# The order of a decoder layer's first splits, some of them on GpSimd, and its last output unit in two halves of 256 columns

## What is computed

```python
h = rmsnorm(x, norm_pre_g)                      # (512, 1024)
u = h @ w_in                                    # (512, 4096): dq, dk, dv, dg, mq, mk, mv, mg, 512 columns each
a = subln(diff_attention(dq, dk, dv)) * silu(dg)   # 4 heads, two softmax maps each, relative bias
b = moba_attention(mq, mk, mv) * silu(mg)          # 8 heads, two blocks of 256, relative bias
y = concat(a, b) @ w_out                        # (512, 1024)
out = x + rmsnorm(y, norm_post_g)
```

## Time and profile before

| | |
|---|---|
| Median of 3 runs | 281.91 us (280.83 to 282.24) |
| Profiled execution, first to last instruction (span) | 280.6 us |
| TensorE busy | 269.3 us, 96% |
| DVE, ScalarE, GpSimd busy | 174.4, 142.8, 29.3 us |
| Granted TensorE clock, mean | 0.994 |

### The profile page before, as it was taken

One profiled execution on the slowest core, in us unless ns is written; L12 is line 12 of the kernel. 1 busy time (PEld: TensorE's weight loads), 2 busy tenths in 40 slices (PEclk: granted clock), 3 DMA queues, 4 the chain that ended last, 5 costly groups with the idle time before them and its releaser, 6 DMA issues.

```text
span 280.6 us, 4661 instructions
## 1 busy us (share of the span) xinstructions
PE 269.3 (96%) x1669; PEld 140.0 (50%) x1669; DVE 174.4 (62%) x383; ACT 142.8 (51%) x335; POOL 29.3 (10%) x76
## 2 busy tenths in 40 slices
PE   6699999999999999999999999999999999999991
PEld 6455444444435555555545445555555565564440
DVE  2685734356777767776876686654687675654423
ACT  2975433266445665557456646574545536442200
POOL 2165000000000000050050130050000000001101
PEclk9999999999999999999999999999999999999997
DMA  7992994258754332204306535224001340101003
GB/s 220 386 317 82 357 386 159 82 139 304 225 188 120 97 99 60 77 7 151 111 2 199 138 112 149 77 78 112 1 2 37 119 183 2 75 2 71 5 25 124
DMA packets 26410, 35.65 MB, mean 127 GB/s; under 512 B 10496, under 2 KB 12808, under 8 KB 26388
## 3 DMA queue, kind: packets, MB, share of 16 engines
q1 hardware_dynamic: 26388, 35.37, 39.0%
HBM read 29.04 MB, written 2.13 MB: 111 GB/s over the span
## 4 chain that ended last, share of the span: by engine, by line
PE 67%; DVE 16%; ACT 9%; issue 4%; DMA 2%; POOL 1%; SPq 0%; DVEq 0%; POOLq 0%; ACTq 0%
PE unit_ps L529 55%; ACT arena L704 4%; PE pt_ps L565 4%; DVE w_lo L785 3%; PE o_ps L583 3%; DVE w_lo L783 2%; DVE pt_lo L880 2%; DMA stage<-in_w_in_dram 2%; PE score_ps L546 2%; DVE arena L854 2%; ACT pt_hi L714 2%; DVE arena L873 2%; PE score_ps L550 2%; PE o_ps L596 1%; ACT junk L643 1%
## 5 line engine op out<-in xcount | busy, mean ns | idle before, releaser
L529 PE MATMUL unit_ps<-w_hi,area 128*128 128x512 f16 x256 | 81.4, 380 | 2.4 <-DVE area L843 1.7
L529 PE MATMUL unit_ps<-area,w_hi 128*128 128x512 f16 x256 | 76.2, 380 | 0.1
L704 ACT ACTIVATE arena<-arena,negmax 128x512 f32<-128x512 f32 (+3 forms) x64 | 35.4, 553 | 61.0 <-DVE negmax L854 61.0
L529 PE MATMUL unit_ps<-area,w_lo 128*128 128x512 f16 x128 | 48.5, 379 | 0.0
L529 PE MATMUL unit_ps<-w_lo,area 128*128 128x512 f16 x128 | 48.5, 379 | 0.0
L880 DVE TENSOR_TENSOR pt_lo<-pt_ps,pt_hi 128x512 f16<-128x512 f32 (+5 forms) x32 | 21.0, 657 | 43.5 <-ACT pt_hi L714 43.5
L529 PEld LDWEIGHTS unit_ps<-w_hi,area 128*128 128x128 f16 x256 | 25.0, 98 | 33.1 <-issue 3.4
L529 PEld LDWEIGHTS unit_ps<-area,w_hi 128*128 128x128 f16 x256 | 24.1, 98 | 26.9 <-issue 0.3
L783 DVE SCALAR_TENSOR_TENSOR w_lo<-stage,g_cols,w_hi 128x512 f16<-128x512 f32 x32 | 25.0, 781 | 7.2 <-ACT w_hi L657 7.1
L854 DVE CUSTOM_DVE_ANT_0 arena<-score_ps,strips 128x512 f32<-128x512 f32 (+3 forms) x64 | 28.5, 482 | 0.0
L529 PE MATMUL unit_ps<-w_hi,q_hi 128*128 128x512 f16 x64 | 24.3, 380 | 0.0
(11 more groups left out here) (84 smaller groups left out, 350.3 us busy)
## 6 DMA issues: line engine op xcount, KB each, us to landing
stage<-in_w_in_dram SPq DMA_DIRECT2D x32, 512.0 KB, 4.5
stage<-in_w_out_dram SPq DMA_DIRECT2D x8, 512.0 KB, 4.3
strips<-bias_rows SPq DMA_DIRECT2D x1, 3072.0 KB, 12.4
arena<-in_x_dram SPq DMA_DIRECT2D x4, 512.0 KB, 8.8
q_twice<-q_hi SPq DMA_DIRECT2D x32, 64.0 KB, 2.7
k_pair<-gates SPq DMA_DIRECT2D x32, 64.0 KB, 2.7
stage<-in_x_dram SPq DMA_DIRECT2D x1, 2048.0 KB, 7.8
out_dram<-area SPq DMA_DIRECT2D x3, 512.0 KB, 2.6
```

Source lines behind the costliest of these rows:

```text
L529: last = nc.tensor.matmul(bank, a, b, start=(k == 0 and n == 0), stop=(k == KT - 1 and n == 2))
L704: nc.scalar.activation(probs[:, i % 2, m, 0:n], neglog[:, i % 2, m, 0:n], ACT.Exp, bias=negmax[:, i, m:m + 1], scale=-1.0, accum_out=sums[ ...
```

## The change

Four things, each within the diff below.

1. ScalarE and DVE do tile 0's `x_hi` and `x_lo` ahead of `split(0)`.
2. GpSimd writes the upper halves of quarters 1 and 3 (`split_hi_part`: two tensor_scalar of 128x512 each), behind its `x_rstd` of tile 0 and tile 1; ScalarE no longer does.
3. ScalarE's `x_hi(1)` moves ahead of `x_square(2)`, and DVE's `x_lo(1)` ahead of `split(3)`.
4. Unit 39 is done as two halves of 256 columns, each 24 matmuls into a bank of `score_ps`, with a square and a weighting for each, and one more small add on GpSimd.

```diff
+    HALF_COLS = WIDTH // 2
+    POOL_SPLITS = [1, 3]
...
+            def split_hi_part(n):
+                g, k = n // 4, 2 * (n % 4)
+                pool.wait_ge(g_scaled, 1)
+                pool.wait_ge(w_loaded[n % 4], 16 * (n // 4 + 1))
+                src = stage[:, n % 4, :].rearrange("p (k n) -> p k n", k=2)
+                for half in range(2):
+                    last = nc.gpsimd.tensor_scalar(w_hi[:, g % 3, k + half, :], src[:, half, :],
+                                                   g_cols[:, k + half:k + half + 1], 1.0, ALU.mult, ALU.mult)
+                last.then_inc(pool_split_hi, 1)
...
                 nc.gpsimd.tensor_tensor(x_rstd[:, t:t + 1], x_ms[:, t:t + 1], minus_half[:, 0:1],
                                         ALU.pow).then_inc(x_rstd_ready, 1)
+                if t < len(POOL_SPLITS):
+                    split_hi_part(POOL_SPLITS[t])
...
+                if t == 0:
+                    pool.wait_ge(y_squared, 2 * TILES + 1)
+                    nc.gpsimd.tensor_tensor(y_last_ms[:, :], y_last_sq[:, :], y_ms[:, 0:1],
+                                            ALU.add).then_inc(y_mean, 1)
+                    pool.wait_ge(y_mean, TILES + 1)
+                    nc.gpsimd.tensor_tensor(y_rstd[:, 0:1], y_last_ms[:, :], minus_half[:, 0:1],
+                                            ALU.pow).then_inc(y_rstd_ready, 1)
+                    break
...
+            def last_unit():
+                _, _, i, g = unit_of(UNITS - 1)
+                pe.wait_ge(logits_ready, 2 * NSTEP)
+                pe.wait_ge(at_ready, 2 * TILES)
+                pe.wait_ge(split_lo, 4 * (g + 1))
+                for half in range(2):
+                    cols = slice(half * HALF_COLS, (half + 1) * HALF_COLS)
+                    for k in range(KT):
+                        wh, wl = w_hi[:, g % 3, k, cols], w_lo[:, g % 3, k, cols]
+                        ah, al = at_hi[:, i % 2, k, :], at_lo[:, i % 2, k, :]
+                        for n, (a, b) in enumerate(((ah, wh), (ah, wl), (al, wh))):
+                            last = nc.tensor.matmul(score_ps[:, half, 0:HALF_COLS], a, b,
+                                                    start=(k == 0 and n == 0), stop=(k == KT - 1 and n == 2))
+                    last.then_inc(last_half_done, 1)
...
             for u, q in FILL_LAST:
-                unit_quarter(u, q)
+                if u < UNITS - 1:
+                    unit_quarter(u, q)
+            last_unit()
...
+                if u == UNITS - 1:
+                    for half, dst in enumerate((y_sq[:, i, r:r + 1], y_last_sq[:, :])):
+                        act.wait_ge(last_half_done, half + 1)
+                        square(dst, score_ps[:, half, 0:HALF_COLS], y_squared, u - IN_UNITS + 1 + half)
+                    return
...
             x_square(0)
-            split(0)
             x_hi(0, 0)
             x_hi(0, 1)
-            split(1)
+            split(0)
             x_square(1)
             split(2)
-            split(3)
+            x_hi(1)
             x_square(2)
-            x_hi(1)
             x_square(3)
...
-                dve.wait_ge(split_hi, n + 1)
+                if n in POOL_SPLITS:
+                    dve.wait_ge(pool_split_hi, POOL_SPLITS.index(n) + 1)
+                else:
+                    dve.wait_ge(split_hi, n + 1 - sum(m < n for m in POOL_SPLITS))
...
+                if u == UNITS - 1:
+                    for half in range(2):
+                        dve.wait_ge(y_squared, u - IN_UNITS + 1 + half)
+                        ycols = slice(r * WIDTH + half * HALF_COLS, r * WIDTH + (half + 1) * HALF_COLS)
+                        nc.vector.tensor_tensor(y_sb[:, i % 2, ycols], score_ps[:, half, 0:HALF_COLS], g_row[:, ycols], ALU.mult)\
+                            .then_inc(y_weighted, 1)
+                    return
...
-            split(0)
             x_lo(0, 0)
             x_lo(0, 1)
+            split(0)
             split(1)
             x_norm(1)
             split(2)
+            x_lo(1)
             split(3)
             x_norm(2)
-            x_lo(1)
             x_norm(3)
```

More of the change, by code:

```diff
@@ L229, in bass_hymba_diff_moba_layer @@
         y_ms = sb("y_ms", [P, TILES])
+        y_last_sq = sb("y_last_sq", [P, 1])
+        y_last_ms = sb("y_last_ms", [P, 1])
         y_rstd = sb("y_rstd", [P, TILES])
@@ L265, in bass_hymba_diff_moba_layer @@
         split_lo = sem("split_lo")
+        pool_split_hi = sem("pool_split_hi")
         consts_ready = sem("consts_ready")
@@ L277, in bass_hymba_diff_moba_layer @@
         unit_done = sem("unit_done")
+        last_half_done = sem("last_half_done")
         unit_read = sem("unit_read")
@@ L916, in finish_rows @@
                 parts = 1 if t else 2
-                dve.wait_ge(y_weighted, 2 * (i + 1))
+                dve.wait_ge(y_weighted, 2 * (i + 1) + (t == 0))
                 dve.wait_ge(y_rstd_ready, i + 1)
```

## The result

The changed kernel took 284.87 us (median of 4 executions, 283.58 to 287.61) against 281.77 before (median of 4): a ratio of 1.0127, 95% interval 1.0094 to 1.0161. The ratio is that of the means (285.23 and 281.65); the medians alone give 1.0110. It is slower, as forecast, but by nearly twice the size: +3.1 us between the medians, where +1.75 was forecast, and by the ratio twice the forecast 283.7 / 281.91 = 1.0063. The median is inside the whole forecast range (281.4 to 285.0), and above the 283.2 to 284.5 of the forecast's own case (A). The four executions come in two kinds, and their mean granted clocks tell which: 283.58 and 284.07 at 0.996 and 0.997, 285.67 and 287.61 at 0.990 and 0.986. The profiled execution is the 285.67 one; its span is 283.9.

A forecast was written before the change was run, and what follows sets the result against it. TensorE sets the time in the long middle, leaving only start and tail open. +2.0 at the start - 0.22 at the tail gave about +1.75 on the 280.6 span, 282.4, plus 1.3 to the median: 283.7 us, range 281.4 to 285.0.

The forecast's parts named there:

- (A): The prediction's own case for the whole kernel: slower, 283.2 to 284.5 us; chance 0.50.
- chain in front of q3: At the start, T1, x_hi(1), x_lo(1) and split(3) run one behind the other: 4.7 us from T1 to q3.
- q3: Last of the four quarters of unit 0 on TensorE; forecast to start at 19.15 and take 1.3 us.
- T1: Transposes of x's tile 1 on TensorE, between unit 0's second and third quarters; forecast at 14.4, as before.
- (D): Rival: the clock falls in the new gap ahead of q3 at the start; 285.0 us or so, chance 0.08.
- q0: First of the four quarters of unit 0 on TensorE; forecast to start at 11.4 with GpSimd and DVE contending.
- collisions: At the start, GpSimd's split_hi_part and DVE's w_lo or x_norm wait for each other, taking back the 0.8 us at T1.
- head start: At the start, without contention, T1 would come at 13.6, 0.8 us earlier than before.
- The tail: Behind the last matmul, ScalarE squares 256 columns instead of 512: gain 0.22 us, between 0 and 0.3.
- (B): Rival: GpSimd and DVE don't meet at the start; +1.1 - 0.22, 282.8 us, chance 0.17.
- (C): Rival: T1 comes at 13.6 and q3 isn't late; -0.8 - 0.22, 280.8 us, chance 0.10.
- (E): Rival: the start's delay is absorbed, leaving only the tail's gain and noise; 281.7 us, chance 0.15.

The follow-up runs named there:

- both stands filled: Changed kernel with 16 warm-up matmuls instead of 8 and split(3) ahead of x_lo(1) on DVE: 283.07 us against 282.42 before, ratio 1.0035.
- the one ahead of q0 filled alone: Changed kernel with 16 warm-up matmuls instead of 8 behind tile 0's transposes: 283.98 us against 282.18 before, ratio 1.0087.
- the one ahead of q3 shortened alone: Changed kernel with split(3) ahead of x_lo(1) on DVE: 282.79 us against 282.18 before, ratio 1.0039.
- GpSimd's halves alone: Kernel before with only the upper halves of quarters 1 and 3 moved from ScalarE to GpSimd: 282.69 us against 282.42, ratio 1.0020.
- x first alone: Kernel before with only tile 0's x_hi and x_lo ahead of split(0) on ScalarE and DVE: 282.03 us against 282.42, ratio 0.9993.

## Why the prediction was right in its mechanism and short in its size

**The chain in front of q3: right, and it is the whole constant loss.** T1 to q3 was 4.73 for 4.7, T1 to unit 1 6.91 for 6.95. The moves of `x_hi(1)` and `x_lo(1)` alone give 6.97, and 284.03 against 282.34. Swapping the one pair on DVE back in the changed kernel takes 1.2 us off.

**The step that failed: T1 at 14.4 "as before", at a full clock.** The prediction took the clock to be at 1.00 until the tail. Its rival (D) saw a fall only in the gap between q2 and q3, with a chance of 0.08, and it didn't price the other stand, the one ahead of q0. Its own walk put q0 at 11.4, some 2 us behind the last warm-up, and it said nothing of that; the kernel before had stood 1.7 us there at a full clock. In the profiled execution the stand became 2.08, the clock was 0.50 from 12.0 to 15.3, and T1 came at 15.86, 1.4 us late. At most 0.8 of that is the clock (T1's input was ready at 15.08); the other 0.6 is `x_norm(1)`, held up by x_rstd and by GpSimd's half in an execution whose loads landed 0.6 to 0.7 us later than before. So two of the signs named were missed, T1 between 13.6 and 14.9 and unit 1 between 20.5 and 21.9 (22.77); the gap ahead of q3, 2.16, was in its range. Four of ten executions show a lower mean clock and lie 1.0 to 3.6 us above the median of the other six; the medians' difference of 3.1 us, where 1.75 was forecast, is this and the scatter of four executions.

**What is shown of the clock, and what isn't.** That a longer stand ahead of q0 makes a lower mean oftener is shown in the kernel before (7 of 12 executions without the warm-ups, 4 of 90 with them). In the changed kernel it is 4 of 10, and 0 of 12 with both stands filled; with the one ahead of q0 filled alone it is 1 of 6, with the one ahead of q3 shortened alone 2 of 12 (one of them at 0.993). The long stand ahead of q3 in the old kernel gives 1 of 16 (both runs of that pair). That points to the stand ahead of q0, but it doesn't separate the two in the changed kernel. Where the stand ahead of q0 is 1.71 in the profile, with x first and no halves on GpSimd, it is 0 of 30 (three runs). One run doesn't fit: GpSimd's halves alone, with the old order up to q0, gave 3 of 12. Only one execution with a fall in the start was profiled, and it also had later landings, and those can delay T1 by themselves (at a full clock, with the changed order up to T1, it is at 13.64 where tile 1 landed 6.7 us behind its issue, and at 14.11 and 14.25 where that took 7.4; here it took 8.3). No run holds the landings fixed, so how much of the 1.0 to 3.6 us is the clock stays open. An estimate for the slowest execution: 0.986 against the 0.997 of the others over 285.8 us is 3.1 us of full-speed time, so even there the clock need not be all of the 3.6.

**GpSimd against DVE: the rule right, its weight too large.** 0.69 for 0.75 each, turns taken as forecast, `x_norm(1)` held up as forecast. But the prediction gave the collisions 0.9 of its 2.0 us, and taking GpSimd out of the changed kernel won 0.2. The walk through the queues used one execution's landings; in another the first pair ran before DVE wanted the port. The prediction also said that ScalarE's relief "buys little", and it is worth about what the collisions cost.

**The constant part: right in size, in part by luck.** It is +1.8 for +1.75, and the chain gives 1.93 us by itself (6.91 against 4.98). At T1 the prediction set a head start of 0.8 against collisions that ate it. The head start is there at the landings that it went by (13.72 for 14.43, without GpSimd), but it turns into a loss at earlier ones, and x first alone is 0.9993 of the time of before; the collisions net of ScalarE's relief are 0.2. The two errors go against each other. Two sums of the prediction are slightly off and change nothing: the floor for T1 adds up to 12.94, not 12.98, and the gap ahead of q3 by its own walk is 19.15 - 16.2 - 1.3 = 1.65, not 1.8.

**The tail: right.** Forecast -0.22, in the profile 0.18 less 0.08. Too small for the time to show.

**The rivals.** (B), no collision, would be 282.8, and isn't it: at a full clock without GpSimd the time was 283.8. (C), the head start wins, is out, as T1 to unit 1 never fell below 6.9 with `x_lo(1)` in front. (E), absorbed, is out by the same runs. (D) had a fall of the clock, but in the gap ahead of q3; in the one fall profiled it came behind q0's stand, and the clock was 1.00 from 16.98 to 20.59.

## What to carry to other kernels

When a wait is moved forward in an in-order queue, count what stands behind it: `x_lo(1)` was ready to be made earlier and wasn't needed before unit 1, but in front of `split(3)` it made q3 wait for a transpose, a copy and a subtraction of another tile. A change that makes a stand of TensorE a few tenths longer should be priced with the lower clock behind it as well as without (one stand of 2.08 us had it, one of 2.93 didn't), and the mean granted clock of each execution read beside its time, since the median can hide two kinds. And a walk through the queues worked out from one execution's landings holds for that execution; the distance between two steps of one queue, T1 to unit 1, held: 4.98 or 4.97 in all five undisturbed profiles with the old order behind T1 and no halves on GpSimd, 6.91 or 6.97 in all five with the new one.

## What the runs showed of the hardware

A tensor_scalar of 128x512, float32 to float16, takes GpSimd 0.69 us alone, a little less than DVE's `w_lo` of the same size. Side by side the two engines took turns by the instruction, each instruction that waited at 1.1 to 1.2 us. And the clock at the start isn't the same in every execution: in the repeated run of the changed kernel the transposes of tile 0 took 1.97 us and the warm-ups behind them 2.75, instead of 1.09 and 1.95. The clock record of that execution begins 10.3 us into the span, and that of the kernel before at 4.4, so the rise to the full clock came later there; the windows before the record's start read 1.00, and the mean of 0.995 doesn't tell it.
